# A hybrid decoder layer on one core: h's halves side by side in the first feed-forward layer, masked products grouped, bonus and zero fill moved

## What is computed

```
h = RMSNorm(x);  P = h @ w_in                      # 1024 x 6912, feeds three mixers and the gates
mixer A: RWKV-7, 8 heads x 64: a recurrent state per head, here computed in chunks of 128 tokens (blocks) of 64
         o += sum(r * k * r_k) * v                 # the "bonus"
mixer B: causal attention with QK-norm;  mixer C: pooling over windows 2, 4, 8, 16
x = x + (sum of gated branches) @ w_out
h2 = RMSNorm(x)
x = x + square(relu(h2 @ w_ff1)) @ w_ff2           # 1024 x 4096 and 4096 x 1024
```

## Time and profile before

| | |
|---|---|
| Median of 3 runs | 466.96 us (466.77 to 468.04) |
| Profiled execution | 467.01 us, its span 465.2 us |
| TensorE busy | 459.6 us of the span, 3660 matmul passes |
| VectorE busy | 295.0 us |
| ScalarE busy | 245.8 us |
| GpSimd busy | 33.1 us |
| Read from memory | 75.30 MB |
| Granted TensorE clock, mean | 1.000 |

### The profile page before, as it was taken

The page is one execution under the profiler, slowest core; times in us unless marked ns, Lnnn a source line. Parts: engine busy times, 40 slices in busy tenths (PEclk is TensorE's granted clock), DMA queues, the critical chain, the costliest instruction groups (busy, mean ns, idle before and its releaser), DMA issues.

```text
span 465.2 us, 8736 instructions
## 1 busy us (share of the span) xinstructions
PE 459.6 (99%) x3660; PEld 397.7 (85%) x3660; DVE 295.0 (63%) x405; ACT 245.8 (53%) x370; POOL 33.1 (7%) x41
## 2 busy tenths in 40 slices
PE   8999999999999999999999999999999999999997
PEld 4999986788977778788888889999999999999995
DVE  4675998674564766766778758655555555555542
ACT  5597655646555456566543538444444444444430
POOL 2000100021670001002000000000000000000000
PEclk9999999999999999999999999999999999999999
DMA  7776635533424435445656564655556656565602
GB/s 235 235 231 217 220 96 177 151 122 93 145 87 136 118 110 142 130 159 171 189 185 184 175 193 143 209 184 184 184 189 194 197 184 182 185 182 190 204 10 90
DMA packets 48694, 76.91 MB, mean 165 GB/s; under 512 B 2576, under 2 KB 28944, under 8 KB 48656
## 3 DMA queue, kind: packets, MB, share of 16 engines
q1 hardware_dynamic: 48656, 76.36, 53.1%
HBM read 75.30 MB, written 1.05 MB: 164 GB/s over the span
## 4 chain that ended last, share of the span: by engine, by line
PE 90%; DVE 3%; ACT 2%; DMA 2%; issue 1%; POOL 1%; DVEq 0%; ACTq 0%
PE bank L497 26%; PE bank L498 25%; PE bank L499 25%; DMA stage<-in_w_in 2%; PE bank L606 1%; PE bank L762 1%; PE bank L743 1%; DVE w_lo L1142 1%; PE bank L638 1%; ACT w_hi L900 1%; POOL small L1472 1%; DVE xs L1458 1%; PE bank L626 1%; PE bank L829 1%; PE bank L793 1%
## 5 line engine op out<-in xcount | busy, mean ns | idle before, releaser
L1142 DVE TENSOR_TENSOR w_lo<-stage,w_hi 128x1024 fp32r<-128x1024 f32 x138 | 167.9, 1225 | 89.1 <-ACT w_hi L900 89.1
L900 ACT CAST w_hi<-stage 128x1024 fp32r<-128x1024 f32 x138 | 144.5, 1052 | 109.5 <-PE bank L499 88.6
L497 PE MATMUL bank<-h_hi,w_hi 128*128 128x256 f32 x384 | 109.8, 286 | 0.3 <-DVE h_lo L1386 0.3
L498 PE MATMUL bank<-h_lo,w_hi 128*128 128x256 f32 x384 | 108.6, 283 | 0.0
L499 PE MATMUL bank<-h_hi,w_lo 128*128 128x256 f32 x384 | 108.6, 283 | 0.0
L497 PEld LDWEIGHTS bank<-h_hi,w_hi 128*128 128x128 f32 x384 | 73.6, 192 | 1.6 <-issue 0.8
L498 PEld LDWEIGHTS bank<-h_lo,w_hi 128*128 128x128 f32 x384 | 73.6, 192 | 0.6
L499 PEld LDWEIGHTS bank<-h_hi,w_lo 128*128 128x128 f32 x384 | 73.6, 192 | 0.0
L497 PE MATMUL bank<-w_hi,h_hi 128*128 128x512 f32 x144 | 60.4, 420 | 0.0
L497 PE MATMUL bank<-w_hi,r_hi 128*128 128x512 f32 x144 | 56.4, 392 | 0.0
L499 PE MATMUL bank<-w_hi,h_lo 128*128 128x512 f32 x144 | 56.4, 391 | 0.0
(11 more groups left out here) (231 smaller groups left out, 541.9 us busy)
## 6 DMA issues: line engine op xcount, KB each, us to landing
stage<-in_w_ff SPq DMA_DIRECT2D x64, 512.0 KB, 3.8
stage<-in_w_in SPq DMA_DIRECT2D x54, 512.0 KB, 3.8
stage<-in_w_branch SPq DMA_DIRECT2D x12, 512.0 KB, 4.5
stage<-in_w_out SPq DMA_DIRECT2D x8, 512.0 KB, 4.1
xs<-in_x SPq DMA_DIRECT2D x2, 512.0 KB, 3.9
out<-xs SPq DMA_DIRECT2D x4, 256.0 KB, 2.1
cst<-in_consts SPq DMA_DIRECT2D x1, 608.0 KB, 6.6
att<-in_w SPq DMA_DIRECT2D x1, 256.0 KB, 5.9
```

Of the source, the lines that this page charges most:

```text
L497: pe.matmul(o, lh, rh, start=first, stop=False)
L498: pe.matmul(o, lh, rl, start=False, stop=False)
L900: nc.scalar.copy(w_hi[:, v % RING], stage[:, v % STAGES]).then_inc(hi_done, 1)
L1142: dve.tensor_tensor(w_lo[:, v % RING], stage[:, v % STAGES], w_hi[:, v % RING].bitcast(F32), ALU.subtract)\
```

## The change

It has four parts.

1. `h_hi` and `h_lo` become two halves of one tensor `h_two`. In an ff1 unit each of 16 groups is now one matmul of 512 columns, the high weights against both halves of h, into a whole bank, and one of 256 columns, the low weights against the high half, added to the second half of that bank. Each ff1 unit fills two banks, one for each half of 128 channels. These are fixed: 6 and 7 for even units, 4 and 5 for odd ones, and the last transposes of h2 get banks 4 and 5.
2. The end of an ff1 unit changes: VectorE adds the two halves of each bank (one `tensor_reduce` each), then makes max(f, 0) x f in one instruction; ScalarE copies this into `r_hi` at part 0 of the next unit; VectorE makes `r_lo` at part 1 of the next unit, between that unit's two weight splits.
3. Both groups of a block's masked products come at one place: block 0 at (8, 2) (before (8, 0) and (8, 2)), block 1 at (9, 2) (before (9, 0) and (9, 2)). The places of `xt_c` and of its transpose stay. The bonus goes from (8, 1) to (10, 0), on TensorE and on VectorE.
4. The zero fill on ScalarE goes from (7, 2) to (6, 3).

```diff
-PROD_AT = {(8, 0): (0, 0), (8, 2): (0, 1), (9, 0): (1, 0), (9, 2): (1, 1)}
+PROD_AT = {(8, 2): 0, (9, 2): 1}
+BONUS_AT = (10, 0)
...
-                    use(("ff", u[1]), dense=True)
+                    for j in range(2):
+                        use(("ff", u[1], j), 6 - 2 * (u[1] % 2) + j, dense=j == 1)
...
-        out += [(("h2", 2 * h2_place(t, p) + i),) for i in range(2)]
+        out += [(("h2", 2 * h2_place(t, p) + i), 4 + i) for i in range(2)]
...
-        h_hi = sb("h_hi", [P, KD, T], F32R)
-        h_lo = sb("h_lo", [P, KD, T], F32R)
+        h_two = sb("h_two", [P, 2, KD, T], F32R)
+        h_hi, h_lo = h_two[:, 0], h_two[:, 1]
...
+                if u[0] == "ff1":
+                    name = ("ff", u[1], i)
+                    o = room(pe, name) if p < 2 else ps(name)
+                    cols = slice(P * i, P * i + P)
+                    for kk in range(4):
+                        k = 4 * (p // 2) + kk
+                        if k % 2 == 0 and u == ("ff1", 0) and i == 0:
+                            copied(pe, ("h2", k // 2))
+                        pe.matmul(o[:].rearrange("p (s t) -> p s t", s=2), wh[:, kk, cols], h_two[:, :, k],
+                                  start=k == 0, stop=False)
+                        ins = pe.matmul(o[:, T:2 * T], wl[:, kk, cols], h_hi[:, k], start=False, stop=k == KD - 1)
+                    if p == 2:
+                        ins.then_inc(full_of(name), 1)
...
-                if (t, p) == (8, 1):
+                if (t, p) == BONUS_AT:
                     pe.wait_ge(rk_ready, 1)
...
                 if (t, p) in PROD_AT:
-                    products(*PROD_AT[t, p])
+                    for g in range(2):
+                        products(PROD_AT[t, p], g)
...
-                if (t, p) == (7, 2):
+                if (t, p) == (6, 3):
                     copied(act, ("kb", 0))
                     act.wait_ge(zero_ready, 2)
...
+                if p == 0 and UNITS[t - 1][0] == "ff1":
+                    i = UNITS[t - 1][1]
+                    act.wait_ge(sq_ready, i + 1)
+                    if i >= 2:
+                        act.wait_ge(used, 2 * (UNITS.index(("ff2", i - 2)) + 1))
+                    nc.scalar.copy(r_hi[:, 2 * (i % 2):2 * (i % 2) + 2], fsq[i % 2].rearrange("p (k t) -> p k t", k=2))\
+                      .then_inc(f_hi, 1)
...
-                    c, g = PROD_AT[t, p]
-                    if g == 0:
-                        dve.wait_ge(mask_in, 16)
-                    for e in range(2):
+                    c = PROD_AT[t, p]
+                    dve.wait_ge(mask_in, 16)
+                    for g, e in ((0, 0), (0, 1), (1, 0), (1, 1)):
...
+                if p == 1 and UNITS[t - 1][0] == "ff1":
+                    i = UNITS[t - 1][1]
+                    b = 2 * (i % 2)
+                    dve.wait_ge(f_hi, i + 1)
+                    rest(r_lo[:, b:b + 2], fsq[i % 2].rearrange("p (k t) -> p k t", k=2), r_hi[:, b:b + 2])\
+                        .then_inc(f_ready, 1)
...
+                    for j in range(2):
+                        o = take(dve, ("ff", i, j))
+                        dve.tensor_reduce(ffs[i % 2][:, T * j:T * j + T], o[:].rearrange("p (s t) -> p t s", s=2), AX_X, ALU.add)\
+                           .then_inc(drained_of(("ff", i, j)), 1)
+                    for j in range(2):
+                        copied(dve, ("ff", i, j))
+                    dve.scalar_tensor_tensor(out=fsq[i % 2], in0=ffs[i % 2], scalar=0.0, in1=ffs[i % 2],
+                                             op0=ALU.max, op1=ALU.mult).then_inc(sq_ready, 1)
```

More of the change, by code:

```diff
@@ L202, in pe_uses @@
     if (t, p) in PROD_AT:
-        out += [(("prod", *PROD_AT[t, p], e),) for e in range(2)]
+        out += [(("prod", PROD_AT[t, p], g, e),) for g in range(2) for e in range(2)]
     if (t, p) in FIRST_X_AT:
@@ L257, in dense_ends @@
         if u[0] == "ff1":
-            ends[("ff", u[1])] = 2 * t + 2
+            ends[("ff", u[1], 1)] = 2 * t + 2
     return ends
@@ L426, in build_layer @@
         ss2_ready, h2_hi = sem("ss2_ready"), sem("h2_hi")
-        f_hi, f_ready = sem("f_hi"), sem("f_ready")
+        sq_ready, f_hi, f_ready = sem("sq_ready"), sem("f_hi"), sem("f_ready")
         fin_ready, stored = sem("fin_ready"), sem("stored")
@@ L539, in part @@
                 i = p % 2
-                if u[0] in ("feat", "ff1"):
-                    name = ("unit", t) if u[0] == "feat" else ("ff", u[1])
+                if u[0] == "ff1":
[11 more added lines that the diff above has]
+                        ins.then_inc(full_of(name), 1)
+                elif u[0] == "feat":
+                    name = ("unit", t)
                     if p == 0:
@@ L548, in part @@
                         k = 4 * (p // 2) + kk
-                        if k % 2 == 0 and u == ("ff1", 0) and i == 0:
-                            copied(pe, ("h2", k // 2))
                         ins = mm3(o[:, T * i:T * i + T], wh[:, kk, cols], wl[:, kk, cols], h_hi[:, k], h_lo[:, k],
@@ L1091, in finish @@
                       .then_inc(drained_of(("unit", t)), 1)
[L1092 to L1102, removed]
             for t in range(SLOTS):
```

## The result

The changed kernel takes **470.28 us** (469.3 to 470.8, 5 runs), the kernel before 467.5 us (466.77 to 468.04, 5 runs, the first three of them those shown above). The ratio is 1.0058 with a 95% interval of 1.004 to 1.0076: slower by 2.7 us. I had forecast 466.5, in a range up to 469.3.

The account below looks back on a forecast made before the run. TensorE was taken to bound the kernel, with VectorE arriving together with it at the `xt_c` transpose. 467.0 - 3.2 (ff1 passes) + 2.8 (moved work) gave 466.5 us, rounded down; forecast 465.6 to 467.8, range 464.5 to 469.3.

Parts of the forecast that it names:

- The wait and the moved work: Before block 0's `xt_c` transpose: TensorE waits 3.7 us, starts 0.1 later; products add 1.0, bonus 1.75: +2.8 us.
- Part 1: In ff1, 256 groups of one 512-column and one 256-column pass replace three 256-column passes: -3.2 us.
- alternation that gains nothing: Rival in ff1: alternating widths keep a group at 0.36 us, giving 469.8 us, halfway 468.2; chance 0.15.
- The clock: Rival at the new wait before the `xt_c` transpose: clock falls, losing 1.5 to 3.1 us, 468.0 to 469.6; chance 0.12.
- the other rivals: No wait: 463.0 (0.10); cheap widths: 464.9 (0.10); alternation gaining nothing: 469.8 (0.15); wait at ff1's new end: above 469 (0.03).
- Part 2: At the end of an ff1 unit, the new VectorE and ScalarE work lies beside TensorE: 0 us.
- Part 4: ScalarE's earlier zero fill falls into a DMA gap and removes the bonus's wait, some 0.35 to 0.45 us.
- its term for the bonus: Bonus moved to (10, 0): 2.20 us less its wait of 0.35 to 0.45, so +1.75 us.
- No wait before the transpose: Rival at block 0's `xt_c` transpose: VectorE's masks come in time, moved work is only moved; 463.0 us, chance 0.10.

Follow-up runs that it names:

- run 5: The whole change plus 14 throwaway 512-column passes on TensorE ahead of its wait for block 0's `xt_c`, against the kernel before: 468.04 us, ratio 1.0022.
- run 1: The feed-forward parts of the change alone, with masked products, bonus and zero fill where they were, against the kernel before: 465.69 us, ratio 0.996.
- run 8: run 7 with passes sorted by width in every ff1 unit but the first, 512 columns then 256 for each piece; against the kernel before: 463.88 us, ratio 0.9945.
- run 9: run 8 with the second piece of an ff1 unit in opposite order, 256-column passes first; against the kernel before: 463.17 us, ratio 0.9911.
- run 2: The moves alone (grouped products, bonus at (10, 0), zero fill at (6, 3)) on the kernel before: 471.43 us, ratio 1.0084.
- run 7: run 1 with the zero fill at (6, 3) instead of (7, 2), against the kernel before: 465.12 us, ratio 0.9962.
- run 10: The whole change with the zero fill back at (7, 2), against the kernel before: 470.79 us, ratio 1.0073.
- run 4: The whole change with the bonus back at (8, 1), against the kernel before: 466.67 us, ratio 0.9985.
- run 3: The whole change with the transpose of block 0's `xt_c` at (9, 3) instead of (9, 1), against the kernel before: 468.11 us, ratio 1.0016.
- run 6: The whole change with VectorE's four masks of block 0 ahead of the split of piece 22, against the kernel before: 467.8 us, ratio 1.0017.

## Why the prediction was wrong, point by point

- **The wait and the moved work: right.** Its sum was +2.8 us, with the transpose at 79.8 after a wait of 3.7. Measured: 79.78, 3.78 and 2.7, and 2.77 in run 5 with the clock at full speed. All three came out of the earlier trace rows: VectorE's fixed order, the duration of a mask, and the landing of a DMA.
- **Part 1: the mechanism right, the size off.** The term was -3.2 us, by 0.227 + 0.120 for a group, and measured -1.75 in the trace and -1.9 by run 1. The bounds had the truth in them (0.24 + 0.12 at the dear end, 0.34 at the cheap end), and I took the middle because two observed switches added up to 0.35. The step that failed is this: I took a single switch for the steady state of alternation. The two single switches were read rightly (233 and 113 ns, together 346), but in the changed kernel's alternating units the next pass starts 236 ns behind one of 512 columns and 117 behind one of 256, on average, together 353. The same step had a rival of its own, alternation that gains nothing, with 0.354 as the mark: the 0.353 measured lies just short of it. The starts in the ff2 units had more to say. Behind the 256-column stream the passes of 512 are 233, 236, 228, 233 and 230 ns apart before they settle at 227, 27 ns too many in all, while the way back gains 7 once. A stream that alternates never settles. Runs 8 and 9 show that the order of the widths costs this, by sorting.
- **The clock: the rival that came true, with too small a chance.** I gave 0.12 to the fall of the clock, at 1.5 to 3.1 us. The mean clock was 0.991 to 0.996 in all five runs of the change and in all five of run 2. In the profiled execution of the change it was down for 3.41 us, which cost 1.34; run 5 shows that filling the wait prevents it. I had taken a length of 6.2 us from the warming passes, for which the earlier trace rows has 6.77. The Trainium skill (TensorE: Matmul & The Clock Gate, section HAM oscillation — how this bites in real kernels) warns that idle gaps between bursts of matmuls send the clock down; the trace agrees, with 3.2 us without a pass ahead of the fall. What I should have done is to make it a term of the sum as soon as I had worked out a wait of 3.7 us, and to take the other rivals against that. 467.5 + 2.7 - 1.75 + 1.34 = 469.8, and the median of 470.28 has the runs in which the clock was down longer. Half a microsecond of the distance to the forecast is no term of it: I started from 467.0, the median of three runs, and five give 467.5.
- **Part 2: right at 0 us.** TensorE has no wait in the feed-forward part, and the 1.75 us that the trace gives back there are what the distance of the passes alone makes (256 x 0.0069 = 1.8).
- **Part 4: 0 us as far as the runs can tell**, each to 0.6 us (runs 7 and 10). The traces lean to a gain of about 0.5, of which the sum had the bonus's wait of 0.4 in its term for the bonus.
- **No wait before the transpose**: didn't happen.

So two errors of the same sign, about 1.4 us each, added to a sum whose large terms nearly cancelled. A sum of -3.2 and +2.8 should have had a wider range than either term alone.

## What to carry to other kernels

Before moving work on the busiest engine ahead of or behind a point where it waits for another, work out when that other engine gets there: work moved behind a fixed point is added in full, and the room that it leaves is a wait. A wait of a few microseconds on TensorE can then cost twice, since the passes behind it may run at half the clock, as those behind 3.78 us did here; throwaway passes can fill it (468.04 us), though a better order was worth more (466.67 in run 4). Where passes of two widths have to be issued, sort them by width: it is free, and it made the same work 1.5 us shorter here.

## What the runs showed of the hardware that I had not expected

- The distance between fp32r passes is 227 ns for 512 columns and 120 for 256 in a steady stream, and 353 for a pair that alternates, 6 ns more than the two. After a change from 256 to 512 the distance takes five passes to settle at 227 (233, 236, 228, 233 and 230 ns ahead of that).
- The granted clock went to 0.50 in a wait of 3.78 us (the change, 3.41 us long), and also in one of 2.74 (run 3, 6.83 us long). In the profiled execution of run 6 it went to 0.50 for 3.41 us behind a wait of 2.20, and only half a microsecond after the passes had started again (11.55, then 12.06), while a wait of 2.6 later in the same execution left it at 1.00. Two waits of 1.4 and 1.1 us with work between them (run 4) left it at full speed in the profile. So the length of the wait alone doesn't tell whether the clock falls.
- The clock can be down for another reason than the wait looked at: besides that execution of run 6, one of run 8, which has no such wait in its profile, had a mean of 0.996 and was 0.9 to 2.8 us above the others, and one of the eight of the kernel before that were taken beside runs 9 and 10 had 0.996 and 470.0 us, 2.2 to 3.1 above the rest. The mean granted clock beside each time tells such executions apart from an effect of the edit.
